# Second block's mixers: the first gate queued behind the projection, latents turned inside linear attention, rotation ahead of the sums, the branch sum turned by halves

## The reference, cut to what matters

```
for l in range(DEPTH):
    x = x + 0.5 * swiglu_2(rms_norm_2(x, ffn1_norm[l]), ffn1_w1[l], ffn1_w3[l], ffn1_w2[l])
    h = rms_norm_2(x, mix_norm[l])
    z = h @ w_in[l]
    (na_q, na_k, na_v, gq, gk, gv, gr, gfl, gbl, c_q, c_kv, k_rope, gates) = split_cols(z, IN_SPLITS)
    ...
    y_na = neighborhood_attention(qa, ka, va, na_rpb[l])
    o_gla = gla_bidirectional(gq, gk, gv, g_f, g_b)
    y_gla = rms_norm_2(o_gla, gla_out_norm[l]) * jax.nn.silu(gr)
    y_mla = mla_attention(c_q, c_kv, k_rope, ...)     # latents through w_uq and w_ukv, norms, rotation, softmax
    gt = jax.nn.sigmoid(gates.reshape(B, S, N_BRANCH, D))
    mixed = gt[:, :, 0] * (y_na @ w_br_na[l]) + gt[:, :, 1] * (y_gla @ w_br_gla[l]) + gt[:, :, 2] * (y_mla @ w_br_mla[l])
    x = x + mixed @ w_out[l]
    x = x + 0.5 * swiglu_2(rms_norm_2(x, ffn2_norm[l]), ffn2_w1[l], ffn2_w3[l], ffn2_w2[l])
```

## Time and profile before

| | |
|---|---|
| median of 3 runs | 2252.11 us (2247.29 to 2254.12) |
| profiled execution, its own time | 2257.41 us |
| its span | 2255.2 us, 26837 instructions |
| PE, PEld busy | 2091.5 us, 1700.8 us |
| DVE, ACT, POOL busy | 1259.5 us, 1035.2 us, 142.0 us |
| chain that ended last | PE 51%, issue 6%, DVE 3%, ACT 2%, POOL 1% |
| HBM | 153 GB/s over the span |
| mean granted TensorE clock | 0.961 |

### The profile page before, as it was taken

How to read it: one execution, slowest core, us unless ns; L and a number is a source line. 1 busy time by engine, 2 the same in 40 slices (tenths; PEclk the granted TensorE clock), 3 DMA queues, 4 the chain that set the end, 5 groups by cost and what they waited for, 6 DMA issues and landing times.

```text
span 2255.2 us, 26837 instructions
## 1 busy us (share of the span) xinstructions
PE 2091.5 (93%) x9932; PEld 1700.8 (75%) x9932; DVE 1259.5 (56%) x1807; ACT 1035.2 (46%) x1619; POOL 142.0 (6%) x148
## 2 busy tenths in 40 slices
PE   5988799999879999999989889999999989988999
PEld 4875688877768878887767677887887767767887
DVE  3656555566655555555655655555445575655554
ACT  3545554455554444445453445444443545444443
POOL 0000000000000000000301200000000311110000
PEclk9988899999989999999989899999999989999999
DMA  7430355554235555554532445555555453424553
GB/s 249 143 123 10 122 175 187 191 167 139 76 116 187 191 186 163 187 192 152 171 116 71 149 131 169 187 187 168 189 190 180 124 183 98 140 94 156 186 191 102
DMA packets 247639, 346.11 MB, mean 153 GB/s; under 512 B 28180, under 2 KB 177496, under 8 KB 247512
## 3 DMA queue, kind: packets, MB, share of 16 engines
q1 hardware_dynamic: 245272, 340.24, 46.6%
q10 hardware_dynamic: 1696, 2.89, 0.4%
q0 software_dynamic: 544, 1.29, 0.2%
HBM read 343.32 MB, written 2.33 MB: 153 GB/s over the span
## 4 chain that ended last, share of the span: by engine, by line
PE 51%; issue 6%; DVE 3%; ACT 2%; POOL 1%; ACTq 0%; DVEq 0%; POOLq 0%
PE bank L643 16%; PE bank L645 15%; PE bank L644 15%; PE bank L1209 1%; DVE w_lo L472 1%; PE bank L578 1%; POOL o_buf L2328 1%; ACT w_hi L484 0%; DVE x L1308 0%; PE bank L2610 0%; PE bank L2653 0%; ACT h_hi L1350 0%; PE bank L2659 0%; PE bank L1068 0%; POOL rs L784 0%
## 5 line engine op out<-in xcount | busy, mean ns | idle before, releaser
L472 DVE TENSOR_TENSOR w_lo<-raw,w_hi 128x2048 fp32r<-128x2048 f32 (+5 forms) x465 | 738.9, 1606 | 424.7 <-ACT w_hi L484 424.3
L643 PE MATMUL bank<-w_hi,h_hi 128*128 128x512 f32 (+4 forms) x1936 | 774.5, 400 | 77.9 <-ACT h_hi L1350 20.4
L644 PE MATMUL bank<-w_lo,h_hi 128*128 128x512 f32 (+4 forms) x1936 | 759.3, 392 | 0.0
L645 PE MATMUL bank<-w_hi,h_lo 128*128 128x512 f32 (+4 forms) x1936 | 759.3, 392 | 0.0
L484 ACT CAST w_hi<-raw 128x2048 fp32r<-128x2048 f32 (+5 forms) x465 | 617.0, 1351 | 272.5 <-PE bank L645 259.2
L643 PEld LDWEIGHTS bank<-w_hi,h_hi 128*128 128x128 f32 x1936 | 375.7, 194 | 162.6 <-issue 37.4
L645 PEld LDWEIGHTS bank<-w_hi,h_lo 128*128 128x128 f32 x1936 | 375.5, 194 | 74.0
L644 PEld LDWEIGHTS bank<-w_lo,h_hi 128*128 128x128 f32 x1936 | 376.4, 194 | 68.2
L643 PE MATMUL bank<-w_hi,ff_hi 128*128 128x512 f32 x528 | 206.1, 390 | 0.0
L645 PE MATMUL bank<-w_hi,ff_lo 128*128 128x512 f32 x528 | 205.5, 389 | 0.0
L644 PE MATMUL bank<-w_lo,ff_hi 128*128 128x512 f32 x528 | 205.4, 389 | 0.0
(11 more groups left out here) (266 smaller groups left out, 1624.1 us busy)
## 6 DMA issues: line engine op xcount, KB each, us to landing
raw<-in_ffn_w SPq DMA_DIRECT2D x176, 512.0 KB, 4.6
raw<-in_w_in SPq DMA_DIRECT2D x52, 1024.0 KB, 5.2
raw<-in_ffn_w SPq DMA_DIRECT2D x44, 1024.0 KB, 4.9
raw<-in_ffn_wg SPq DMA_DIRECT2D x44, 512.0 KB, 3.9
raw<-in_ffn_wu SPq DMA_DIRECT2D x44, 512.0 KB, 5.0
raw<-in_ffn_wd SPq DMA_DIRECT2D x22, 1024.0 KB, 4.8
raw<-in_od_w_in SPq DMA_DIRECT2D x12, 1024.0 KB, 5.2
raw<-in_w_out SPq DMA_DIRECT2D x8, 1024.0 KB, 5.0
```

Source lines behind the costliest of these rows:

```text
L472: dve.tensor_tensor(lo_[:, cs], raw_[:, cs], hi[:, cs].bitcast(F32), ALU.subtract).then_inc(*dve_did.up())
L643: pe.matmul(out, x_hi, u.hi[:, k, cols_], start=start, stop=False)
L644: pe.matmul(out, x_hi, u.lo[:, k, cols_], start=False, stop=False)
L645: return pe.matmul(out, x_lo, u.hi[:, k, cols_], start=False, stop=stop)
```

## The change

Per layer, in the second block only:
- **Gate 0** is queued ahead of neighborhood attention (`start_gates(after)`), behind the rest of the projection. Gate 1 is cut in two: its first chunk (8 steps) is queued behind branch 0, its second follows the query projection in `latent`, and the weight order follows. `GLA_FILLS` goes from (4, 8, 16, 4, 8) to (4, 8, 12, 4).
- **Linear attention**: the states come ahead of the score products, and PE waits for GpSimd alone there; `latent_turn` (turning of the latents, rotation and copy of the shared key) stands between the score products and the output products. The norm's result goes to `gain` instead of `tmp`, and its turning is returned as a function, which `latent` calls after `w_ukv`.
- **Rotation**: q's squares are taken right after its projection; gain and rotation follow the key-value projection, ahead of the turning of linear attention's result. Both parts of q are then turned together.
- **Branches 1 and 2**: `both_tiles` lets both token tiles do the first two blocks, then both the next two, with a wait for each pair of blocks. Branch 2 may start when the first group of latent attention is done.
- **Sum**: the first half is turned after the first chunk of branch 2 and two steps of the second; then come the rest of the branch, four steps of the output product, the turning of the second half, and the rest.

```diff
-GLA_FILLS = (4, 8, 16, 4, 8)
+GLA_FILLS = (4, 8, 12, 4)
...
-        units += gates[1] + gemm_units(a["mla_w_uq_2"][l], chunked(MLA_H * MLA_QK))
+        half = len(gates[1]) // 2
+        units += gates[1][:half] + gemm_units(a["mla_w_uq_2"][l], chunked(MLA_H * MLA_QK)) + gates[1][half:]
...
+        def both_tiles(h, k0, u, nk, c, n, pair, there, evac):
+
+            tiles = [tile_steps(tt, h, k0, u, nk, c, n, pair, there, evac) for tt in range(TT)]
+            while True:
+                for steps in tiles:
+                    if next(steps, None) is None:
+                        return
+                    yield True
...
+                    if by_block and c == chunks[0][0]:
+                        yield from both_tiles(h, k0, u, nk, c, n, pair, ready.upto, evac)
+                        k0 += u.shape[0]
+                        continue
...
+            start_gates(after)
             attention(groups, flat(o_buf[:, 0, :]), after, lambda i: (4, 3))
             y_there = attended["o"]
-            while fillers:
-                fill()
+            assert len(fillers) == 1
             prepare()
             rstd_heads(*((z[:, :, ZC[name]:ZC[name] + 2 * P].unsqueeze(2), r, 1, 2 * P,
                           sq[:, :, m * 2 * P:(m + 1) * 2 * P]) for m, (name, r) in enumerate(
                               (("cq", rs[:, 24:26]), ("ckv", rs[:, 26:28])))))
-            start_gates()
             start_branch(0, y_there)
-            start_gates()
+            start_gates(after, chunked(D)[0:1])
...
                 def _(pe):
                     pe.wait_ge(*bank.drained)
-                    pe.wait_ge(*before.act)
-                    pe.wait_ge(*before.dve)
                     pe.wait_ge(*before.pool)
                     for pr in range(NP2):
...
+            turned_ahead = latent_turn(l, begun)
             before = marks()
             fill(GLA_FILLS[3])
-            og = tmp[:, :, 0:512]
+            og = gain[:, 0, :].rearrange("p (t n) -> p t n", t=TT)
...
+            gated = marks()
+            return *turned_ahead, lambda: to_T(4, lambda b, tt: og[:, tt, b * P:(b + 1) * P], hi_of(y_hi), dst_lo=hi_of(y_lo),
+                                       scale=lambda b: cols[:, 1, gc:gc + 1], after=gated)
...
+        def latent_turn(l, after):
+
             split = []
+            for name, c, hi_, lo_ in (("cq", ZC["cq"], cq_hi, cq_lo), ("ckv", ZC["ckv"], oT_lo[:, 0:2, :], oT_lo[:, 2:4, :])):
                 gc = col_of[(name, l)] % P
+                to_T(2, lambda b, tt: z[:, tt, c + b * P:c + (b + 1) * P], lambda b, n: hi_[:, b:b + n, :],
+                     dst_lo=lambda b, n: lo_[:, b:b + n, :], scale=lambda b: cols[:, 1, gc + b:gc + b + 1], after=after)
                 split.append(marks())
...
+            kr_turned = turn_rope(l, kr.unsqueeze(2), 1, 1, Marks(after.pe, kr_squared, after.dve, after.pool),
+                                  z[:, :, 1344:1472])
 
             @block.gpsimd
             def _(pool):
+                pool.wait_ge(*pe_did.now())
+                pool.wait_ge(*act_did.now())
                 pool.wait_ge(*kr_turned)
...
+            gemm(blocks_of(cq_hi, cq_lo, 2), 2, chunked(MLA_H * MLA_QK),
                  to_sbuf(lambda tt, c, n: q[:, tt, c:c + n], rs_of(24)), split[0])
             q_there = marks()
...
+            start_gates(split[0], chunked(D)[1:2])
+            while fillers:
+                fill()
...
+            gemm(blocks_of(oT_lo, oT_lo[:, 2:4, :], 2), 2, chunked(MLA_H * (MLA_NOPE + MLA_V)), evac_kv, split[1])
             kv_there = marks()
+            turn_rope(l, qv[:, :, :, MLA_NOPE:MLA_QK], MLA_H, 0, Marks(q_there.pe, q_squared, q_there.dve, q_there.pool),
+                      kT[:, :, :].rearrange("p (t a) n -> p t (a n)", t=TT))
+            q_turned = marks()
+            linear_there = turn_linear()
             start_branch(1, linear_there)
-            start_gates()
+            start_gates(split[0])
             prepare()
...
-            start_branch(2, attended["o"])
-            while fillers:
-                fill()
+            start_branch(2, Ready([attended["outs"][0], attended["o"]], 2))
...
-            latent(l, gated_linear(l))
-            by_half = [Marks(pe_did.now(), act_did.now(), dve_did.now(), mixed[(TT - 1, c)]) for c in (0, 512)]
-            acc = out_banks()
-            for k0, after in zip((0, KD // 2), by_half):
-                groups, steps = half_of_o(k0, after)
+            last.clear()
+            latent(l, *gated_linear(l))
+            o = attended["o"]
+            while (TT - 1, 0) not in last:
+                fill()
+            fill(2)
+            turned = []
+            for k0 in (0, KD // 2):
+                groups, steps = half_of_o(k0, Marks(o.pe, o.act, o.dve, last[TT - 1, k0 * P]))
                 for _ in steps:
                     pass
-                for _ in out_steps(acc, h_in, k0, groups[-1], add_x):
-                    pass
+                turned.append(groups[-1])
+                if k0 == 0:
+                    while fillers:
+                        fill()
+                    acc = out_banks()
+                    products = out_steps(acc, h_in, 0, turned[0], add_x)
+                    for _ in range(4):
+                        next(products)
+            for _ in products:
+                pass
+            for _ in out_steps(acc, h_in, KD // 2, turned[1], add_x):
+                pass
```

More of the change, by code:

```diff
@@ L664, in _ @@
                 def _(pe):
-                    if there is not None and (ka == 0 or ka == KD // 2):
+                    if there is not None and (ka == 0 or there(k0 + ka + step) is not there(k0 + ka)):
                         turned = there(k0 + ka + step)
@@ L2287, in _, with start_gates @@
                 act.activation(dst, src, ACT.Silu).then_inc(*act_did.up())
-        gate_there, gate_used, mixed = {}, {}, {}
-        def start_gates():
-            before = marks()
+        gate_there, gate_used, mixed, last = {}, {}, {}, {}
+        def start_gates(before, chunks=chunked(D)):
             def gates(tt, c, n, bank, full):
@@ L2303, in gates @@
                 bank.drained = gate_there[(tt, c)] = act_did.now()
-            fillers.append(gemm_steps(h_in, KD, chunked(D), gates, before))
+            fillers.append(gemm_steps(h_in, KD, chunks, gates, before))
         def start_branch(i, ready):
@@ L2329, in mix @@
                 gate_used[(tt, c)] = mixed[(tt, c)] = pool_did.now()
-            fillers.append(gemm_steps(y_in, 4, chunked(D), mix, ready))
+                if i == 2:
+                    last[tt, c] = pool_did.now()
+            fillers.append(gemm_steps(y_in, 4, chunked(D), mix, ready, isinstance(ready, Ready)))
         def project(l, ready):
@@ L2399, in gated_linear @@
             lowT = kT[0:GLA_RANK + 1, 6:8, :]
-            before = marks()
+            before = begun = marks()
             @block.sync
@@ L2686, in gated_linear @@
             gc = col_of[("gla_out", l)] % P
-            return to_T(4, lambda b, tt: og[:, tt, b * P:(b + 1) * P], hi_of(y_hi), dst_lo=hi_of(y_lo),
-                        scale=lambda b: cols[:, 1, gc:gc + 1], fills=GLA_FILLS[4])
-        def latent(l, linear_there):
-            start = marks()
-            while fillers:
-                fill()
-            q = z[:, :, 0:MLA_H * MLA_QK]
-            kv = z[:, :, ZC["gq"]:ZC["gq"] + MLA_H * (MLA_NOPE + MLA_V)]
-            both = (("cq", ZC["cq"], MLA_H * MLA_QK, q), ("ckv", ZC["ckv"], MLA_H * (MLA_NOPE + MLA_V), kv))
+            gated = marks()
@@ new lines, in gated_linear, with turn_rope, _ @@
+            return *turned_ahead, lambda: to_T(4, lambda b, tt: og[:, tt, b * P:(b + 1) * P], hi_of(y_hi), dst_lo=hi_of(y_lo),
+                                       scale=lambda b: cols[:, 1, gc:gc + 1], after=gated)
+        def turn_rope(l, v, heads, m, before, work):
+            @block.vector
+            def _(dve):
+                dve.wait_ge(*before.pe)
+                dve.wait_ge(*before.act)
+                dve.wait_ge(*before.dve)
+                dve.wait_ge(*before.pool)
+                for tt in range(TT):
+                    dve.tensor_tensor(v[:, tt], v[:, tt], rgain[:, l * 2 + m, :].unsqueeze(1).broadcast_to(
+                        [P, heads, MLA_ROPE]), ALU.mult).then_inc(*dve_did.up())
+            after = Marks(before.pe, before.act, dve_did.now(), before.pool)
+            rotate(v, heads, MLA_ROPE // 2, C("cos2", (TT,)), C("sin2", (TT,)), work, after)
+            return dve_did.now()
```

155 lines of the change are left out of this document (69 added, 86 removed).

## The result

| | before | after |
|---|---|---|
| median of 4 runs | 2251.88 us (2247.29 to 2254.12) | 2275.16 us (2274.09 to 2279.94) |
| profiled execution, span | 2257.4 us, 2255.2 us | 2275.4 us, 2272.8 us |
| PE busy, mean granted clock | 2091.5 us, 0.961 | 2113.9 us, 0.950 |

The ratio is 1.0098, 95% interval 1.0073 to 1.0122: 1.0% slower, where 0.4% faster was predicted. The profiled execution of the kernel before (2257.41 us) lies above all four of its runs, so the two profiles differ by 18.0 us where the medians differ by 23.3. The first thing to see is in the last line of the table. PE is busy 22.4 us longer on the same computation, while the span grew by 17.6 us: PE stands idle *less* than before and still loses. The time went into matmuls at the lower clock.

What follows compares the result with a forecast made beforehand. TensorE was taken as the bound, losing time only when idle or at lower clock. 9.3 - 7.3 - 0.9 - 2.0 + 5.6 = 4.7 us per layer, 9.4 us in all, gave 2243 us (0.4% faster), range 2226 to 2257.

Steps and rivals of the forecast that it cites:

- sum: All five terms added: 4.7 us gained per layer, 9.4 us over both mixers.
- D: Rotation moved ahead of the branch sums: its 4.2 us hole closes, a 6.7 us hole opens at the second branch; net -2.0 us.
- B: Linear attention, states first and latents turned inside: a 7.8 us hole opens ahead of the output products; net -7.3 us.
- C: Linear attention's norm under the latent projections: a 6.3 us hole opens in the gate's third weight unit; net -0.9 us.
- A: Gate queued ahead of neighborhood attention: 1.3 and 6.8 us holes close, 0.8 us stays at the low-rank turn; gain 9.3 us.
- E: Tail, last branch started early and sum turned by halves: waits of 1.4, 1.0, 1.6 and 1.6 us close; +5.6 us.
- Rival 2: The tail gives nothing, since GpSimd's sum or the next weight unit is late: 2254 us; chance 0.20.
- The clock: Work behind a large PE hole runs at the lower clock, costing 2.0 us more than the hole itself.
- Rival 3: PE's clock doesn't come back between the holes in linear attention and the gate's third unit: slower, 2263 us; chance 0.12.
- The sign of being wrong: PE's clock in the mixers ending below 0.90 would show the forecast wrong.
- The range: Whole kernel's time expected between 2226 and 2257 us; the forecast's own range was 2236 to 2250.

Runs made afterwards that it cites:

- e11: e8 with the marks of the low-rank turn taken ahead of its filler steps; 2224.45 us, ratio to before 0.9863.
- e4: Kernel before with only gate 0 queued ahead of neighborhood attention, nine instead of sixteen filler steps in the third place; 2249.16 us, ratio 0.9984.
- e6: Kernel after with the marks for linear attention's output products taken ahead of the turns of the latents; 2269.32 us, ratio to before 1.0057.
- e5: Kernel after with the first gate's third weight unit split ahead of linear attention's norm chain on DVE; 2272.34 us, ratio to before 1.0072.
- e10: Kernel after with e5's early split, e6's earlier marks, and linear attention's output turned ahead of the rotation; 2247.45 us, ratio to before 0.9968.
- e3: Kernel before with only the tail: branch 2 started by the first group, sum turned by halves; 2243.71 us, ratio 0.9953.
- e1: Kernel after with three filler steps moved from inside latent attention to ahead of its score products; 2259.69 us, ratio to before 1.0024.
- e9: Kernel after with latent attention's marks ahead of the filler steps, four steps there instead of two, fewer in its second half; 2248.80 us, ratio to before 0.9969.
- e2: Kernel before with its two filler steps ahead of latent attention's score products moved behind them; 2277.5 us, ratio 1.0109.
- e8: Kernel after with e10's three edits of order and e9's cover of the score products together; 2224.20 us, ratio to before 0.9859.

## Why the prediction was wrong

The step that failed is the **sum**: 4.7 us per layer is carried unchanged from the end of D to the end of the program. Nothing was costed between the turns of the keys and the end of latent attention, since the change doesn't edit that code. There the kernel after loses 12.9 us in the first mixer. What the prediction asked of B, C and D (what is late next on DVE?) it did not ask one step further, where two unchanged filler steps had left PE a wait of just 0.92 us in the kernel before.

| part, us per layer | predicted | first mixer measured |
|---|---|---|
| A | +9.3 | +6.0 |
| B | -7.3 | -4.6 |
| C | -0.9 | -0.8 |
| D | -2.0 | -1.7 |
| turns of the keys to end of attention | 0 | -12.9 |
| E | +5.6 | +6.1 |
| sum | +4.7 | -7.9 |

The measured column is the difference of the two timelines between the same instructions of PE, with filler steps that changed sides counted at 1.36 us; each timeline is one execution, and a row of it can be off by a microsecond. The second mixer, from the last probability turns of neighborhood attention to its end, is 226.2 instead of 216.0 us: -10.2. Both together are 18.1, against 18.0 between the profiled executions; the 5 us by which the medians differ more are in no row.

- **A** was too large by 3.3 us. The hole left ahead of the low-rank turn is 2.2 us and not 0.8, and behind it the clock is at the lower level for part of the stretch (0.84 over the 21.77 us of the window above). The turn waits for this row, a whole weight unit, which the prediction had spread over the steps before it:

```profile
1155.68 2.29 DVE L473 TENSOR_TENSOR w_lo<-raw,w_hi 128x2048 fp32r<-128x2048 f32 x1 [0.85 <-ACT w_hi L485]
```

  Mending the marks there (e11) gained nothing: the waits behind it grew. e4 has the part by itself; its gain of 4.7 us by the medians (ratio 0.9984) hides the 7 us lost in the second mixer's score products, and its first mixer gained 6.8.
- **B**: the hole is there with the releaser that was named, GpSimd's copy of the key, 6.1 instead of 7.8 us. From the end of the turns to the end of that copy it is 15.4 instead of 16.2 us, and PE has 8.7 instead of 8.3 us of work and one more wait of 0.7 us in that time. e6 shows that the copy is waited for without need: the wait ended 3.8 us sooner, and 4.4 us came back in the layer.
- **C and D** were right in place, releaser and size (6.5 for 6.3, 6.3 for 6.7 us). e5 and e10 show that C's hole is DVE's order, down to 3.8 us; what holds the rest wasn't tested. D's wait is an `issue` row, which names no releaser, but DVE's timeline has the low halves behind the rotation, and PE resumes at 1260.76, after the first two of these four:

```profile
1259.78 1.66 DVE L635 SCALAR_TENSOR_TENSOR y_lo<-bank,cols,y_hi 128x256 fp32r<-128x256 f32 x4
```

- **E** was right: no wait over 1 us in the tail but the 1.9 us for the last `h_hi`, and e3 gives it alone, 10.2 us for 11.2 predicted. Rival 2 is out.
- **The clock**: a hole was priced at its length plus 2.0 us, from one stretch in which the dense matmuls of weights follow. That nearly held for the holes of B, C and D, behind which the work took 1.8, 1.8 and 2.7 us longer than at full clock. It failed where score products follow: 8.4 us in them and 2.6 us behind (8.29 against 5.74). Rival 3 named the lower clock and the right sign but looked for it between the holes of B and C, where it wasn't; no chance was given to the unchanged place. The sign of being wrong that the prediction named, a clock in the mixers below 0.90, came up at its edge (0.90 and 0.89).
- **The range** took no rival beyond 2257 us, so a loss of this size had no place in it, not even by rival 3's 2263.

The cause was tested from both sides: shortening that wait to 1.1 us brings back 15.5 us (e1), closing it with marks that don't count the steps' own weight parts 26.4 us (e9); opening one of 2.8 us in the kernel before costs 23.6 us (e2). With that wait covered, the change as it stands is 0.3% faster than before; with the three orders mended too, e8 is 1.4% faster than before and 0.9% faster than the tail alone by the medians (2224.2 and 2243.7).

What is open: why the clock stays at the lower level through score products that keep PE busy without a gap, and what makes it fall. Waits of 0.9 to 1.2 us left the products fast in seven mixers (before, e1, e3, and e4's first), one of 1.2 us (e4's second) did not, one of 2.0 us (e10's second) did, and those of 2.7 us and more did in none of eleven. So the length of the wait alone doesn't decide between 1 and 2 us, and part of a small edit's gain or loss here can be chance.

## What to carry to other kernels

When an edit brings the busiest engine ahead, follow it to the next place where an unedited piece of work only just covered another engine's chain: the gain is spent there first, and what comes behind that wait decides its price. Take the marks of an operation ahead of the filler steps that cover it, or it waits for the preparation of those very steps. If PE's busy time grows with the same instructions, look for the stretch at the lower clock before looking at waits. Compare kernels by their ratios to one that ran beside them, and don't judge an edit of a few microseconds by one profiled execution.

## What the runs showed of the hardware

After a hole of 2.7 to 3.6 us, 32 back-to-back score products (plain f32, 256 columns) ran for 18.4 us at a granted clock of 0.50, 576 ns each instead of 315 (11 mixers in six profiles); the clock was back only in the dense weight matmuls behind them. In the second mixer of e4 it fell to 0.50 behind a hole of 1.2 us, 2.00 us after the products had begun. After a hole of 6.8 us dense weight matmuls had only lost 2.0 us in 7.45. The Trainium skill ("TensorE: Matmul & The Clock Gate", What's actually happening) says that activity releases the throttle; the stretch at 0.50 is 18.44 us of busy PE out of 18.44, so a busy PE in this sense was not enough here. The type f32 alone isn't it either: behind the 6.1 us hole of the kernel after, 16 output products of linear attention, plain f32 with 128 rows and 128 columns, ran at the lower level, and what follows them was at full clock:

```profile
1214.92:1218.59 3.67, 3.67 (x16) 3.46 (x17) 0.00 (x0) 0.00 (x0) 0.00 (x0) 0.51 0.02 4
1218.59:1224.32 5.73, 5.73 (x41) 3.98 (x41) 0.69 (x1) 0.00 (x0) 0.00 (x0) 1.00 0.00 0
```

What differs is the work: in the slow stretch PEld is busy 8.03 of 18.44 us, here 3.46 of 3.67, and half of the score products use 64 rows. Which of it counts was not tried.
